# Two attention heads scored inside the value product, and relative biases asked for one head at a time

## The chip, the cores and the metric

The program runs on one core of a Trainium2 chip. Its time is the device time of one execution in microseconds (us). The kernel before took 2087.86 us, the median of three executions (2085.55, 2087.86 and 2088.91 us).

## The reference, cut to what matters

The model is two blocks one after the other, in f32, on 512 tokens of width 1024. The second block, which is the part that the change touches, has two layers. Each layer is attention, then a gated feed-forward network:

```python
for i in range(2):
    h = rmsnorm(x, norm_mix[i])
    # layer 0: 12 query heads, 4 key and value heads, a window of 128 tokens on either side,
    #          ALiBi slopes as biases and a sink logit per head
    # layer 1: 12 heads of query, key and value, a 16-column window on an 8 x 64 grid,
    #          relative biases rpb from a table
    s = einsum(q, k) * 64 ** -0.5 + bias        # masked outside the window
    y_tok = softmax(s) @ v
    y_mem = softmax(q_mem @ mk) @ mv            # 4 more heads on 256 memory tokens
    x = x + concat(y_tok, y_mem) @ w_out[i]
    h = rmsnorm(x, norm_ffn[i])
    x = x + (silu(h @ w_gate) * (h @ w_up)) @ w_down[i]
```

## The kernel before, in words

**Engines and queues.** Every engine has its own program, and they meet at semaphores. SyncE (SP) starts all DMAs. The weights come as a stream of numbered units, two buffers `raw[0]` and `raw[1]`. ScalarE (ACT) rounds a unit to `w_hi` (`split_hi`, L727), VectorE (DVE) makes the rest `w_lo` (`split_lo`, L1212), and TensorE (PE) multiplies three times for each tile: `w_hi` by `z_hi`, `w_hi` by `z_lo`, `w_lo` by `z_hi` (L1924 to L1936). SP may load unit N when `w_lo` of unit N-2 is done, and ACT may round unit N when PE is through with unit N-2. A unit of `qk` has 24 matmuls of 512 columns.

**Layer of the second block.** The stage `qk` makes queries and keys (10 units in layer 0, 14 in layer 1). ACT copies each unit's result from PSUM (L1143 to L1149), DVE multiplies it by the token's scale (L1776), ACT and DVE split it (L1126, L1788). The stage `v` makes the values: in layer 0 two units, in layer 1 two halves of four units each. Its product (L2405 to L2416) takes 12 matmuls for each of eight k tiles, of 256 columns in layer 0 and 384 in layer 1. At the end of a half ACT and DVE copy two blocks each of the result to `v_tok` (L1161, L1809) and report it on the semaphores `va` and `vd`.

**Attention as a pipeline over heads.** All engines go through `head_steps` (L437), from head 0 to head 18. In step h, PE makes the scores of head h in four blocks (`scores`, L2426, two matmuls a block), turns the exponentials of head h-2 (`turn`, L2440), and multiplies them by the values (`values`, L2451; block 3 of a head falls into the next step). DVE adds the bias, takes the row maximum (`biased`, L1823, a custom instruction and a read of its accumulator), and negates the maxima (`neg_max`, L1896 and L1899). ACT takes the exponentials (L1170) and copies turned blocks to `pts` (L1178). Three PSUM banks go round between the score blocks, so that scores of one block wait until the block three before has been read.

**Where the scores lie.** `ls` (three slots) and two of the three bias slots overlie `z_hi` and `z_lo` (L193 to L195), the operands of the value product. So nothing of the attention but the bias of head 0 can be made before that product is over: GpSimd (POOL) waits for it at L714, and PE's own order puts the first `scores` behind it (L2418 to L2488).

**The biases.** POOL makes one per head, from the slopes in layer 0 (L695) and from the table in layer 1 (L705). For layer 1 SP asks for each head's part of the table with eight DMAs (`bias_load`, L557). The first three heads are asked for in one go, between the second and the third weight unit of `qk1`:

```python
load(n, 0, cols(w, 0))
load(n + 1, 1, cols(w, P))
if l == 1:
    sp.wait_ge(used, n + 2)
    for r in range(3):
        bias_load(r, r)
with sp.Fori(0, qkw // (2 * P) - 1) as i:
    load(n + 2 * i + 2, 0, cols(w, i * (2 * P) + 2 * P))
```

At the start of `qk1` the norm is finished beside the first two units: PE sums squares after the first unit (L2036) and spreads the scale inside the second (L2046), and ACT copies the scale (L788) before it may copy the first results.

Of the kernel before, what the change touches and what calls it, by code (L numbers as in the profile page):

```python
# [12 lines left out]
P = 128  # L13
# [59 lines left out]
def build(nc, t):  # L73
# [3 lines left out]
    with ctx:  # L77
# [21 lines left out]
        minus = sb(fixed, "minus", [P, 4])  # L99
        raw = [sb(fixed, f"raw{i}", [P, SLOT]) for i in range(2)]  # L100
# [64 lines left out]
        at = [scratch + 5 * 4 * T1]  # L165
        mk = sb(at, "mk", [P, 2 * MH, NMEM])
# [23 lines left out]
        bias = [sb([scratch], "bias0", [P, GRID_R * (48 + 32 + 32)])]  # L190
# [3 lines left out]
        ls = [sb(at, f"ls{i}", [P, 4, 3 * P]) for i in range(3)]  # L194
        bias += [sb(at, f"bias{i}", [P, GRID_R * (48 + 32 + 32)]) for i in range(1, 3)]  # L195
# [199 lines left out]

        def y_slot(head):

            return chunked(y_heads[:, head // 2 * 2, :], 4)[:, :, head % 2 * HD:(head % 2 + 1) * HD]
# [38 lines left out]
        def head_steps(eng, step):  # L437


            for h in range(AH + 3):  # L440
                step(h, h % 3, h, h // 3)
# [47 lines left out]
        def _(sp):  # L489
# [114 lines left out]
        def _(pool):  # L604
# [77 lines left out]
            for l in range(2):  # L682
# [8 lines left out]
                def biases(h, g, r):  # L691
                    if l == 0:
                        if h >= 2:
                            pool.wait_ge(*s.at("ls", 4 * h - 8))
                        pool.tensor_tensor(bias[r][:, 0:3 * P], att_con[:, 0:3 * P],  # L695
                                           con[:, bass.ds(cc["slopes"] + h, 1)].to_broadcast([P, 3 * P]),
                                           ALU.mult).then_inc(s["bias"], 1)
                    else:
# [3 lines left out]
                        for v, (first, n) in enumerate(((1, 2), (0, 3), (0, 2))):  # L702
                            x0 = first * BC
                            mask = att_con[:, 3 * P + 48 * v + x0:3 * P + 48 * v + x0 + n * BC]
                            x = pool.tensor_tensor(  # L705
                                bias[r][:, at_:at_ + n * P].rearrange("p (n r c) -> p n r c", n=n, r=GRID_R),
                                rpb_raw[r][:, :, x0:x0 + n * BC].rearrange("p r (n c) -> p n r c", n=n),
                                mask.rearrange("p (n o c) -> p n o c", n=n, o=1)
                                    .to_broadcast([P, n, GRID_R, BC]), ALU.add)
# [16 lines left out]
        def _(act):  # L726
# [386 lines left out]
            def layer(l):  # L1113
# [40 lines left out]
                for half in range((1, 2)[l]):  # L1154
                    count, width = ((2, KVA * HD), (4, 384))[l]
                    for i in range(count - 1):
                        m = count * half + i
                        split_hi(n + m + 2, i % 2, WIDTHS[n + m + 2])
# [5 lines left out]
                    m = count * (half + 1) - 1  # L1164
                    split_hi(n + m + 2, 1, WIDTHS[n + m + 2])

                def exps(h, r, memory, blocks):
                    for b in blocks:
                        lo, width = span(memory, b)
                        act.activation(ls[r][:, b, lo:lo + width], ls[r][:, b, lo:lo + width], ACT.Exp,  # L1170
# [25 lines left out]
                head_steps(act, step)  # L1196
# [14 lines left out]
        def _(dve):  # L1211
# [546 lines left out]
            def layer(l):  # L1758
# [43 lines left out]
                for half in range((1, 2)[l]):  # L1802
                    count, width = ((2, KVA * HD), (4, 384))[l]
                    for i in range(count - 1):
                        m = count * half + i
                        split_lo(n + m + 2, i % 2, WIDTHS[n + m + 2])
# [6 lines left out]
                    m = count * (half + 1) - 1  # L1813
                    split_lo(n + m + 2, 1, WIDTHS[n + m + 2])
# [8 lines left out]
                def biased(h, r, b):  # L1823
# [3 lines left out]
                    dve.tensor_tensor_reduce(ls[r][:, b, lo:lo + width], banks(r + b)[:, 0:width],  # L1827
                                             bias[r][:, at_:at_ + width], 1.0, 3 * NEG, ALU.add, ALU.max,
                                             row_max[r][:, b:b + 1]).then_inc(s["ls"], 1)

                def taken(h, r, b):

                    dve.wait_ge(*s.at("s", 4 * h + (b + 1)))
                    dve.tensor_copy(ls[r][:, b, 0:NMEM], banks(r + b)[:, 0:NMEM]).then_inc(s["ls"], 1)

                def largest(h, r, b):
                    dve.wait_ge(*s.at("ls", 4 * h + (b + 1)))
                    dve.tensor_reduce(row_max[r][:, b:b + 1], ls[r][:, b, 0:NMEM], AX.X, ALU.max)\
                       .then_inc(s["max"], 1)

                def copy(h, memory, b):
# [3 lines left out]
                    dve.tensor_copy(pts[1][:, 0:width], ps[3][:, 1, 0:width]).then_inc(s["pd"], 1)  # L1845

                def step(h, r, n_, g):
# [47 lines left out]
                    if banded and l == 0:  # L1895
                        dve.scalar_tensor_tensor(neg_max[r][:, :], row_max[r][:, :], vec("sink", h), minus[:, :],  # L1896
                                                 ALU.max, ALU.mult).then_inc(s["neg"], 1)
                    elif front:
                        dve.scalar_tensor_tensor(neg_max[r][:, :], row_max[r][:, :], -2.0, row_max[r][:, :],  # L1899
                                                 ALU.mult, ALU.add).then_inc(s["neg"], 1)  # L1900
                head_steps(dve, step)
# [14 lines left out]
        def _(pe):  # L1916
# [473 lines left out]
            def layer(l):  # L2390
# [8 lines left out]
                count, kt, width = ((2, 4, KVA * HD), (4, 2, 384))[l]  # L2399
                for half in range((1, 2)[l]):  # L2400
                    if l == 0 or half:
# [15 lines left out]

                pe.wait_ge(*s.at("scaled", (10, 14)[l]))  # L2418
                pe.wait_ge(*s.at("q_lo", (8, 12)[l]))
                pe.wait_ge(*s.at("zero", 1))  # L2420
                if l:

                    pe.wait_ge(*s.at("va", 1))
                    pe.wait_ge(*s.at("vd", 1))

                def scores(h, r, n_, b, kv):  # L2426
                    memory = n_ >= QH
                    _, width = span(memory, b)
                    bank = banks(r + b)[:, 0:width]
                    if memory:  # L2430
                        x = pe.matmul(bank, q_mem[:, n_ - QH, b * P:(b + 1) * P], mk[:, MH * l + n_ - QH, :],  # L2431
                                      start=True, stop=True)
                    else:
                        lo = key_block(False, b, 0) * P
                        for keys, first in ((k_hi, True), (k_lo, False)):
                            x = pe.matmul(bank, q_pair[:, n_, b * P:(b + 1) * P], keys[:, kv, lo:lo + width],  # L2436
                                          start=first, stop=not first)
                    x.then_inc(s["s"], 1)

                def turn(h, r, memory, b):  # L2440
# [5 lines left out]
                    for j in range(width // P):  # L2446
                        x = pe.transpose(ps[3][:, b % 2, j * P:(j + 1) * P],  # L2447
                                         ls[r][:, b, lo + j * P:lo + (j + 1) * P], ident)
# [39 lines left out]
                head_steps(pe, step)  # L2488
# [109 lines left out]
```

## Time and profile before

| | |
|---|---|
| median of three executions | 2087.86 us |
| the profiled execution | 2088.28 us |
| its span | 2086.5 us |
| PE busy | 2047.6 us, 98% |
| DVE busy | 1091.2 us, 52% |
| ACT busy | 868.2 us, 42% |
| POOL busy | 182.4 us, 9% |
| mean granted clock of TensorE | 0.995 |
| DMA | 28.5% of 16 engines |

The span runs from the first to the last instruction that the profile sees; 1.8 us of the profiled execution lie outside it. In the rows below, a timeline row is: start in us, length in us, engine, line, operation, output from inputs, shape, count, and in brackets the engine's idle time just before it and what ended it. PE is matmuls and PEld the loading of stationary operands. Matmul ends are modelled, so that the next one may start before the end shown.

### The profile page before, as it was taken

To read this page: it belongs to the slowest core of one execution; us is meant where nothing else is said; L and a number is where in the kernel's file an instruction comes from. 1 tells how busy PE (TensorE), PEld (TensorE's weight loads), DVE (VectorE), ACT (ScalarE), POOL (GpSimd) and SP (SyncE) were. 2 spreads that over 40 slices of the span, in tenths; PEclk is the share of its full clock that TensorE was granted. 3 is DMA by queue.
4 is the path that set the end of the run, shared out by engine and by line. 5 is a ranking of instruction groups with operands and counts; after the bars stand their busy time and mean duration, and the time that the engine had idled before them with its cause. 6 is when DMAs were issued, how large, how long until landed. Compare 5 with 4: busy or idle time off the path is not lost.

```text
span 2086.5 us, 32286 instructions
## 1 busy us (share of the span) xinstructions
PE 2047.6 (98%) x11899; PEld 1793.3 (86%) x11899; DVE 1091.2 (52%) x1809; ACT 868.2 (42%) x1350; POOL 182.4 (9%) x177
## 2 busy tenths in 40 slices
PE   8999999999999999999999999999999999999998
PEld 8999999999988988888988888888789888888887
DVE  4234777555662566556764433444555654433443
ACT  5534444543221544456743322234556643322233
POOL 0013000110010000001000100010004001100000
PEclk9999999999999999999999999999999999999999
DMA  4322111133333333332023332332322033333332
GB/s 134 104 81 81 41 42 41 55 88 91 93 103 111 90 90 94 104 106 61 1 71 100 91 111 81 92 104 78 100 83 60 24 91 97 102 93 91 90 102 80
DMA packets 321921, 174.99 MB, mean 84 GB/s; under 512 B 6561, under 2 KB 319137, under 8 KB 321841
## 3 DMA queue, kind: packets, MB, share of 16 engines
q1 hardware_dynamic: 321840, 173.92, 28.5%
q8 instruction: 50, 0.82, 0.2%
q14 instruction: 31, 0.25, 0.0%
HBM read 171.80 MB, written 2.10 MB: 83 GB/s over the span
## 4 chain that ended last, share of the span: by engine, by line
PE 66%; DVE 1%; ACT 1%; DMA 1%; issue 1%; SPq 0%; POOL 0%; POOLq 0%; DVEq 0%; ACTq 0%
PE ps L1928 38%; PE ps L1934 19%; PE ps L2462 3%; PE ps L2414 2%; PE ps L2447 2%; PE ps L2436 1%; PE ps L2431 1%; SPq L561 0%; ACT w_hi L731 0%; PE ps L2496 0%; DVE w_lo L1214 0%; DMA raw<-w_in_a 0%; DMA raw<-w_mem_kv 0%; DMA raw<-w_in_b 0%; PE ps L2297 0%
## 5 line engine op out<-in xcount | busy, mean ns | idle before, releaser
L1928 PE MATMUL ps<-z_hi,w_hi 128*128 128x512 f32 (+2 forms) x2128 | 645.2, 344 | 7.7 <-ACT scaled_heads L1143 5.1
L1928 PE MATMUL ps<-z_lo,w_hi 128*128 128x512 f32 (+2 forms) x2128 | 635.9, 339 | 0.0
L1214 DVE TENSOR_TENSOR w_lo<-raw,w_hi 128x1024 fp32r<-128x1024 f32 (+2 forms) x298 | 384.1, 1289 | 467.5 <-ACT w_hi L731 466.3
L731 ACT ACTIVATE w_hi<-raw 128x1024 fp32r<-128x1024 f32 (+2 forms) x298 | 328.2, 1102 | 428.4 <-PE ps L1934 374.4
L1934 PE MATMUL ps<-z_hi,w_lo 128*128 128x512 f32 (+2 forms) x2128 | 443.8, 339 | 0.0
L1928 PEld LDWEIGHTS ps<-z_hi,w_hi 128*128 128x128 f32 x2128 | 367.2, 189 | 60.4 <-issue 10.4
L1928 PEld LDWEIGHTS ps<-z_lo,w_hi 128*128 128x128 f32 x2128 | 366.0, 189 | 45.0
L1934 PEld LDWEIGHTS ps<-z_hi,w_lo 128*128 128x128 f32 x2128 | 344.2, 188 | 45.3
L1928 PE MATMUL ps<-g_hi,w_hi 128*128 128x512 f32 (+1 forms) x539 | 209.4, 390 | 0.5 <-POOL g_lo L662 0.5
L1928 PE MATMUL ps<-g_lo,w_hi 128*128 128x512 f32 (+1 forms) x539 | 208.8, 389 | 0.0
L662 POOL TENSOR_TENSOR g_lo<-gv,g_hi 128x512 f32 x66 | 85.6, 1297 | 1075.2 <-ACT g_hi L1068 1075.2
L1934 PE MATMUL ps<-g_hi,w_lo 128*128 128x512 f32 (+1 forms) x539 | 147.4, 388 | 0.0
L1559 DVE TENSOR_TENSOR H<-H,ps 128x512 f32<-128x512 f32 (+2 forms) x64 | 44.1, 689 | 178.4 <-PE ps L1934 178.4
L1928 PEld LDWEIGHTS ps<-g_hi,w_hi 128*128 128x128 f32 x539 | 101.1, 188 | 23.9 <-POOL g_lo L662 1.9
L1928 PEld LDWEIGHTS ps<-g_lo,w_hi 128*128 128x128 f32 x539 | 101.2, 188 | 22.1
L1934 PEld LDWEIGHTS ps<-g_hi,w_lo 128*128 128x128 f32 x539 | 99.7, 188 | 21.9
L1068 ACT ACTIVATE g_hi<-gv 128x512 f32 (+1 forms) x66 | 41.7, 632 | 181.2 <-DVE gv L1702 181.2
L1928 PE MATMUL ps<-mix_hi,w_hi 128*128 128x264 f32 (+1 forms) x256 | 76.5, 339 | 0.0
L1928 PE MATMUL ps<-mix_lo,w_hi 128*128 128x264 f32 (+1 forms) x256 | 76.3, 339 | 0.0
L1170 ACT ACTIVATE ls<-ls,neg_max 128x256 f32<-128x256 f32 (+1 forms) x128 | 68.7, 539 | 6.7 <-DVE neg_max L1899 6.7
L2462 PEld LDWEIGHTS ps<-v_tok,pts 128*128 128x128 f32 x480 | 64.8, 192 | 3.1 <-DVE pts L1845 1.2
L2462 PE MATMUL ps<-v_tok,pts 128*128 128x64 f32 x480 | 64.8, 266 | 0.5 <-ACT pts L1178 0.5
(317 smaller groups left out, 2387.8 us busy)
## 6 DMA issues: line engine op xcount, KB each, us to landing
raw<-w_gate_up SPq DMA_DIRECT2D x88, 512.0 KB, 3.7
raw<-w_down SPq DMA_DIRECT2D x48, 704.0 KB, 4.4
raw<-w_in SPq DMA_DIRECT2D x44, 512.0 KB, 3.7
raw<-w_up SPq DMA_DIRECT2D x44, 512.0 KB, 3.7
raw<-w_out SPq DMA_DIRECT2D x24, 512.0 KB, 3.6
raw<-w_in_b SPq DMA_DIRECT2D x14, 512.0 KB, 3.8
raw<-w_in_a SPq DMA_DIRECT2D x12, 512.0 KB, 3.6
raw<-w_branch SPq DMA_DIRECT2D x8, 512.0 KB, 3.6
```

Of the source, the lines that this page charges most:

```text
L662: pool.tensor_tensor(lo, src, hi.bitcast(F32), ALU.subtract).then_inc(done, 1)
L731: act.activation(w_hi[s][:, 0:width], raw[s][:, 0:width], ACT.Copy).then_inc(hi_done, 1)
L1068: act.activation(g_hi[:, j, 0:tokens], gv[:, 0:tokens], ACT.Copy).then_inc(s["hi"], 1)
L1170: act.activation(ls[r][:, b, lo:lo + width], ls[r][:, b, lo:lo + width], ACT.Exp, bias=neg_max[r][:, b:b + 1], accum_out=row_sum[r][:, b:b ...
L1214: dve.tensor_tensor(w_lo[s][:, 0:width], raw[s][:, 0:width], w_hi[s][:, 0:width].bitcast(F32), ALU.subtract).then_inc(lo_done, 1)
L1559: dve.tensor_tensor(tile, tile, more, ALU.add).then_inc(ps_free[s], 1)
L1928: pe.matmul(out, w_hi[s][:, w0 + k * P:w0 + (k + 1) * P], rhs[:, lo:lo + width], start=a, stop=False)
L1934: x = pe.matmul(out, w_lo[s][:, w0 + k * P:w0 + (k + 1) * P], rhs_hi[:, lo:lo + width], start=False, stop=last)
L2414: x = pe.matmul(v_bank(l, half, c)[:, 0:width], zz[:, k, c * P:(c + 1) * P], ww[i % 2][:, kk_ * width:(kk_ + 1) * width], start=a, stop=b)
L2431: x = pe.matmul(bank, q_mem[:, n_ - QH, b * P:(b + 1) * P], mk[:, MH * l + n_ - QH, :], start=True, stop=True)
L2447: x = pe.transpose(ps[3][:, b % 2, j * P:(j + 1) * P], ls[r][:, b, lo + j * P:lo + (j + 1) * P], ident)
L2462: x = pe.matmul(y_bank(r)[:, b * HD:(b + 1) * HD], pts[b % 2][:, j * P:(j + 1) * P], v, start=j == 0, stop=j == width // P - 1)
```

## The change

Scores, bias and maxima of heads 0 and 1 are made inside the value product: PE puts one score block behind each of the eight k tiles (in layer 1 of the second half only), DVE handles the blocks ahead of its weight splits, and ACT takes the exponentials of head 0 ahead of copying the values. The steps of `head_steps` then start with head 2. For that, `ls` slots 0 and 1 and bias slot 1 move to other places, POOL makes the bias of head 1 before the product's end, and in layer 1 PE waits for `va` and `vd` of the first half ahead of the second. In the `qk` stage of layer 1, `bias_load` of heads 0, 1 and 2 goes ahead of the units 4, 6 and 8, one head each. The moves of `ls[r]` to `ls(r, b)` and `bias[r]` to `bias[l][r]` elsewhere are left out here.

```diff
+        tails = [fixed[0] + 4 * SLOT * i + 4 * UNIT for i in (0, 1, 4, 5)]
...
+        first_bias = sb([scratch], "bias0", [P, GRID_R * (48 + 32 + 32)])
+        ls_first = sb([scratch + 2 * 4 * T1], "ls0", [P, 4, 3 * P])
+        ls_second = [sb([tails[b]], f"ls1_{b}", [P, 3 * P]) for b in range(4)]
...
-                load(n, 0, cols(w, 0))
-                load(n + 1, 1, cols(w, P))
-                if l == 1:
-
-                    sp.wait_ge(used, n + 2)
-                    for r in range(3):
-                        bias_load(r, r)
-                with sp.Fori(0, qkw // (2 * P) - 1) as i:
-                    load(n + 2 * i + 2, 0, cols(w, i * (2 * P) + 2 * P))
-                    load(n + 2 * i + 3, 1, cols(w, i * (2 * P) + 3 * P))
+                for i in range(qkw // (2 * P)):
+                    if l == 1 and 2 <= i < 5:
+                        sp.wait_ge(used, n + 2)
+                        bias_load(i - 2, i - 2)
+                    load(n + 2 * i, 0, cols(w, i * (2 * P)))
+                    load(n + 2 * i + 1, 1, cols(w, i * (2 * P) + P))
...
                 biases(0, 0, 0)
+                biases(1, 0, 1)
 
                 pool.wait_ge(used, UNITS[f"out{l}"] + 2)
-                for h in range(1, QH):
+                for h in range(2, QH):
                     biases(h, h // 3, h % 3)
...
+                for half in range((1, 2)[l]):
+                    count, width = ((2, KVA * HD), (4, 384))[l]
+                    final = half == (0, 1)[l]
+                    for i in range(count):
+                        m = count * half + i
+                        if i == count - 1:
+                            if final:
+                                step(1, 1, 1, 0)
+                            values_taken(half, count, width)
+                        split_hi(n + m + 2, i % 2, WIDTHS[n + m + 2])
+                head_steps(act, step, 2)
...
+                def front_blocks(h, blocks):
+
+                    dve.wait_ge(*s.at("bias", h + 1))
+                    dve.wait_ge(*s.at("scaled", 2 * pairs))
+                    for b in blocks:
+                        scored(h, b)
+                        biased(h, h, b)
+                    if 3 in blocks:
+                        dve.wait_ge(*s.at("ls", 4 * h + 4))
+                        negated(h, h)
...
+                for half in range((1, 2)[l]):
+                    count, width = ((2, KVA * HD), (4, 384))[l]
+                    final = half == (0, 1)[l]
+                    for i in range(count):
+                        m = count * half + i
+                        if final:
+                            first = 8 * i // count
+                            front_blocks(first // 4, range(first % 4, first % 4 + 8 // count))
+                        if i == count - 1:
+                            values_taken(half, count, width)
+                        split_lo(n + m + 2, i % 2, WIDTHS[n + m + 2])
+                head_steps(dve, step, 2)
...
                 for half in range((1, 2)[l]):
+                    final = half == (0, 1)[l]
+                    if l and half:
+                        pe.wait_ge(*s.at("va", 1))
+                        pe.wait_ge(*s.at("vd", 1))
...
+                            if final:
+                                h, block = divmod(kt * i + kk_, 4)
+                                if k == 0:
+                                    pe.wait_ge(*s.at("q_lo", (8, 12)[l]))
+                                pe.wait_ge(*s.at("ls", 4 * h + (block - 2)))
+                                scores(h, h, h, block, (0, h)[l])
                         x.then_inc(used, 1)
...
-                head_steps(pe, step)
+                pe.wait_ge(*s.at("scaled", (10, 14)[l]))
+                pe.wait_ge(*s.at("zero", 1))
+                head_steps(pe, step, 2)
```

## Rows read from the trace of the kernel before

**Rows 1.** The page: PE's busy time, and the qk weight loads of layer 1.

```profile
PE 2047.6 (98%) x11899; PEld 1793.3 (86%) x11899; DVE 1091.2 (52%) x1809; ACT 868.2 (42%) x1350; POOL 182.4 (9%) x177
...
raw<-w_in_b SPq DMA_DIRECT2D x14, 512.0 KB, 3.8
```

**Rows 2.** PE's waits, whole span: line, released by; us in total, times, longest.

```profile
PE ps L2436 <- DVE row_max L1827: 5.5, 2, 3.0
```

**Rows 3.** Timeline of the start of qk1, SP, DVE and PE.

```profile
1457.32 11.03 SPq L561 DMA_DIRECT2D rpb_raw<-rpb  x24
...
1460.94 1.23 DVE L1214 TENSOR_TENSOR w_lo<-raw,w_hi 128x1024 fp32r<-128x1024 f32 x1
...
1466.36 1.05 PE L2046 MATMUL ps<-con,stat 128*128 128x128 f32 x8
...
1475.26 0.79 PE L1928 MATMUL ps<-z_hi,w_hi 128*128 128x512 f32 x1 [5.06 <-ACT scaled_heads L1143]
```

**Rows 4.** The chain of waits: start us, us, what, matmuls in it.

```profile
953.94 11.38 PE ps L2414 x96
...
1472.50 1.06 ACT w_hi L731
...
1475.26 6.45 PE ps L1928 x16
...
1483.57 3.69 PE ps L1928 x16
...
1546.58 33.40 PE ps L2414 x189
```

**Rows 5.** Timeline from the end of layer 0's value product.

```profile
965.02 0.19 PEld L2436 LDWEIGHTS ps<-k_hi,q_pair 128*128 128x128 f32 x1
...
965.34 0.88 DVE L1809 TENSOR_SCALAR v_tok<-ps,stat 128x256 f32<-128x256 f32 x2 [3.31 <-PE ps L2414]
...
965.38 1.61 POOL L695 TENSOR_TENSOR bias<-att_con,con 128x384 f32<-128x384 f32 x2 [13.27 <-PE ps L2414]
...
966.06 1.05 ACT L731 ACTIVATE w_hi<-raw 128x1024 fp32r<-128x1024 f32 x1
...
968.77 0.58 PE L2436 MATMUL ps<-k_hi,q_pair 128*128 128x256 f32 x1 [2.54 <-DVE row_max L1827]
...
969.61 0.43 DVE L1827 CUSTOM_DVE_ANT_0 ls<-ps,bias 128x256 f32<-128x256 f32 x1
...
977.19 0.55 PE L2462 MATMUL ps<-v_tok,pts 128*128 128x64 f32 x4
...
981.51 0.55 PE L2462 MATMUL ps<-v_tok,pts 128*128 128x64 f32 x4
```

**Rows 6.** Timeline of layer 1's value product: between the halves, and from its end.

```profile
1562.97 0.88 PE L2414 MATMUL ps<-w_hi,z_hi 128*128 128x384 f32 x4
1563.17 1.14 DVE L1809 TENSOR_SCALAR v_tok<-ps,stat 128x384 f32<-128x384 f32 x2 [2.30 <-PE ps L2414]
...
1579.62 0.19 PEld L2436 LDWEIGHTS ps<-k_hi,q_pair 128*128 128x128 f32 x1
...
1583.90 0.58 PE L2436 MATMUL ps<-k_hi,q_pair 128*128 128x256 f32 x1 [2.98 <-DVE row_max L1827]
...
1592.66 0.55 PE L2462 MATMUL ps<-v_tok,pts 128*128 128x64 f32 x4
```

**Rows 7.** Instructions of L1896: duration ns min/median/max, first and last start.

```profile
L1896 DVE SCALAR_TENSOR_TENSOR neg_max<-row_max,par,minus x12: 223/887/891, 970.1 to 1016.0; 128x4 f32<-128x4 f32 x12
```

**Rows 8.** Table by stretch: us, busy us of each engine, then PEclk, DMA share, GB/s.

```profile
868.00:875.00 7.00, 4.85 (x42) 4.68 (x41) 3.59 (x5) 3.22 (x6) 0.00 (x0) 1.00 0.38 120
...
968.70:972.00 3.30, 3.23 (x10) 2.60 (x10) 3.26 (x16) 1.00 (x4) 0.83 (x1) 0.50 0.54 159
...
1583.90:1586.90 3.00, 3.00 (x11) 2.75 (x12) 2.96 (x14) 1.11 (x5) 3.00 (x5) 0.50 0.23 50
```

**Rows 9.** Timeline of PE in the memory stage.

```profile
870.71 0.36 PE L1928 MATMUL ps<-mz_hi,w_hi 128*128 128x256 f32 x1 [2.15 <-DVE w_lo L1214]
```

More of the change, by code:

```diff
@@ L165, in build @@
         at = [scratch + 5 * 4 * T1]
+        mk_at = at[0]
         mk = sb(at, "mk", [P, 2 * MH, NMEM])
@@ L193, in build @@
         at = [fixed[0] - 2 * 4 * KD * T1]
-        ls = [sb(at, f"ls{i}", [P, 4, 3 * P]) for i in range(3)]
-        bias += [sb(at, f"bias{i}", [P, GRID_R * (48 + 32 + 32)]) for i in range(1, 3)]
+        ls_third = sb(at, "ls2", [P, 4, 3 * P])
+        last_bias = sb(at, "bias2", [P, GRID_R * (48 + 32 + 32)])
+        k_lo_unused = region + 4 * SEQ * (AH + QH + KVA)
+        bias = [(first_bias, sb([(k_lo_unused, mk_at)[l]], f"bias1_{l}", [P, GRID_R * (48 + 32 + 32)]), last_bias)
+                for l in range(2)]
         pts = [sb(at, f"pts{i}", [P, 3 * P]) for i in range(2)]
@@ L435, in key_block, with head_steps @@
             return j if memory else max(b - 1, 0) + j
-        def head_steps(eng, step):
-            for h in range(AH + 3):
+        def head_steps(eng, step, first=0):
+            for h in range(first, AH + 3):
                 step(h, h % 3, h, h // 3)
@@ L692, in biases @@
                     if l == 0:
-                        if h >= 2:
+                        if h >= 3:
                             pool.wait_ge(*s.at("ls", 4 * h - 8))
-                        pool.tensor_tensor(bias[r][:, 0:3 * P], att_con[:, 0:3 * P],
+                        pool.tensor_tensor(bias[l][r][:, 0:3 * P], att_con[:, 0:3 * P],
                                            con[:, bass.ds(cc["slopes"] + h, 1)].to_broadcast([P, 3 * P]),
@@ L1153, in layer, with values_taken @@
                 n = UNITS[f"v{l}"]
[L1154 to L1158, printed above, removed]
+                def values_taken(half, count, width):
                     act.wait_ge(used, n + count * (half + 1) + 2)
@@ L1169, in exps @@
                         lo, width = span(memory, b)
-                        act.activation(ls[r][:, b, lo:lo + width], ls[r][:, b, lo:lo + width], ACT.Exp,
+                        act.activation(ls(r, b)[:, lo:lo + width], ls(r, b)[:, lo:lo + width], ACT.Exp,
                                        bias=neg_max[r][:, b:b + 1], accum_out=row_sum[r][:, b:b + 1])\
@@ L1801, in layer, with values_taken @@
                 n = UNITS[f"v{l}"]
[L1802 to L1806, printed above, removed]
+                def values_taken(half, count, width):
                     dve.wait_ge(used, n + count * (half + 1) + 2)
@@ L1826, in biased @@
                     at_ = (0, 2 * P, 2 * P, 5 * P)[b] if l else lo
-                    dve.tensor_tensor_reduce(ls[r][:, b, lo:lo + width], banks(r + b)[:, 0:width],
-                                             bias[r][:, at_:at_ + width], 1.0, 3 * NEG, ALU.add, ALU.max,
+                    dve.tensor_tensor_reduce(ls(r, b)[:, lo:lo + width], banks(r + b)[:, 0:width],
+                                             bias[l][r][:, at_:at_ + width], 1.0, 3 * NEG, ALU.add, ALU.max,
                                              row_max[r][:, b:b + 1]).then_inc(s["ls"], 1)
@@ L1894, in step @@
                         dve.wait_ge(*s.at("max", 4 * (n_ - QH) + 4))
[L1895 to L1901, printed above, removed]
+                    if front:
+                        if banded:
+                            negated(h, r)
+                        else:
+                            dve.scalar_tensor_tensor(neg_max[r][:, :], row_max[r][:, :], -2.0, row_max[r][:, :],
+                                                     ALU.mult, ALU.add).then_inc(s["neg"], 1)
+                for half in range((1, 2)[l]):
[10 more added lines that the diff above has]
+                head_steps(dve, step, 2)
                 for k in range(KD):
@@ L2399, in layer, with scores @@
                 count, kt, width = ((2, 4, KVA * HD), (4, 2, 384))[l]
+                def scores(h, r, n_, b, kv):
+                    memory = n_ >= QH
+                    _, width = span(memory, b)
+                    bank = banks(r + b)[:, 0:width]
+                    if memory:
+                        x = pe.matmul(bank, q_mem[:, n_ - QH, b * P:(b + 1) * P], mk[:, MH * l + n_ - QH, :],
+                                      start=True, stop=True)
+                    else:
+                        lo = key_block(False, b, 0) * P
+                        for keys, first in ((k_hi, True), (k_lo, False)):
+                            x = pe.matmul(bank, q_pair[:, n_, b * P:(b + 1) * P], keys[:, kv, lo:lo + width],
+                                          start=first, stop=not first)
+                    x.then_inc(s["s"], 1)
                 for half in range((1, 2)[l]):
+                    final = half == (0, 1)[l]
+                    if l and half:
+                        pe.wait_ge(*s.at("va", 1))
+                        pe.wait_ge(*s.at("vd", 1))
                     if l == 0 or half:
@@ L2415, in layer @@
                                                   ww[i % 2][:, kk_ * width:(kk_ + 1) * width], start=a, stop=b)
-                        x.then_inc(used, 1)
[L2418 to L2438, printed above, removed]
+                            if final:
[4 more added lines that the diff above has]
+                                scores(h, h, h, block, (0, h)[l])
+                        x.then_inc(used, 1)
                 def turn(h, r, memory, b):
```

24 lines of the change are left out of this document (14 added, 10 removed).

## The prediction

> **What bounds the kernel now.** I read the page first. PE is busy for 98% of the span and no other engine for more than 52% [rows 1], so only what gives PE its idle or slow time back can move the end. Next come PE's waits: the longest kind is the first scores of attention behind DVE's row maxima, 5.5 us in two places, one per layer [rows 2], then one wait of 5.06 us at the start of qk1 [rows 3]. The timelines around these three places say what stands in the way, and the chain of waits and the table by stretch say what the clock did there: after each of the three idle times PE runs for some microseconds at half of its full clock (granted 0.50, that is 1.2 instead of 2.4 GHz) [rows 4, 8].
>
> **Start of qk1.** SP spends 11.03 us on 24 asks for relative biases [rows 3], 3.7 us a head. They are queued ahead of the third weight unit, which lands when ACT starts rounding it, at 1472.50 [rows 4]. PE starts on it at 1475.26 after 5.06 us idle, and its first 16 matmuls take 6.45 us where the next unit's take 3.69 [rows 3, 4]. They end at 1481.71.
>
> In the new order the third and fourth unit are asked for first. The third is asked for before the stage begins, the fourth at 1462.2, when the second unit's w_lo is done [rows 3]; each lands 3.8 us later [rows 1], so the DMA is early. What is late next is ACT: it copies the scale after PE has spread it, which ends at 1467.41 [rows 3]. From 1472.50 to 1475.26 ACT rounds (1.06), copies the scale and copies two heads [rows 4, 3]: 2.76 us, of which 1.70 follow the rounding. The rounding now fits ahead of the spread, so PE's bank is free at 1467.41 + 1.70 = 1469.1. PE is through with the second unit at 1470.0 (its modelled end is 1475.26 - 5.06 = 1470.20, and its next matmul can start a little earlier). So PE doesn't stop, the clock stays up, and the 16 matmuls end at 1470.0 + 3.7 = 1473.7. Gain 1481.7 - 1473.7 = **8.0 us**.
>
> The 24 asks don't vanish. Each group of eight (3.7 us) now stands on SP between unit 3 and 4, 5 and 6, 7 and 8. Between two loads of the stream lie about 5.5 us (24 matmuls at 3.69/16 = 0.231 us), so 3.7 us fit in. Even if a load went out late by all of 3.7 us, it would land 7.5 us after its release, and PE needs it only two units (11.1 us) less a split of about 2.5 us after the unit two before is through. I cost this at nothing; without that cover it would be 3.7 us less slack for each load, up to a few microseconds. POOL needs the first bias only at the end of qk1, 80 us on. The unrolled loop on SP costs nothing that PE sees.
>
> **Ramp of attention, layer 0.** Now the value product ends at 965.02, PE makes three score blocks and then stands for 2.54 us until DVE has copied the values, split a unit and freed a bank [rows 5]. Then DVE and ACT have to go through head 0 and head 1 before values can be multiplied, at half clock on PE. The steady state is visible in block 3 of the values: 977.19 for head 0, 981.51 for head 1, so 4.32 us a head [rows 5].
>
> Afterwards eight score blocks (16 matmuls) lie inside the product. By width one matmul takes 11.38/96 = 0.119 us at 256 columns and 33.40/189 = 0.177 us at 384 [rows 4], so a head's scores take 1.18 us, both 2.36. This work is moved, not added. The product's last matmul is issued by 965.02 + 2.36 - 0.24 = 967.14 (the last score block, 0.24, comes behind it). Call this E. At E + 0.35 ACT, DVE and POOL are released, as at 965.34 to 965.38 now [rows 5]. ACT copies (till E + 1.2) and rounds (1.05, till E + 2.3). DVE must first do the last block of head 1 (starts at E + 0.45, 0.43 and a read), then its neg_max, then the value copies of 0.88. POOL starts two biases at E + 0.36, 0.8 us each [rows 5], and neg_max takes 0.22 us alone but 0.89 beside such a bias in nearly all of its instances [rows 7]. I let it end with POOL's first bias, at E + 1.25; the bounds are E + 1.1 and E + 2.0 (behind the second one). The values are then there at E + 2.2, and PE starts step 2 there; step 2 waits for them at its head. From there to block 3 of head 0's values PE has one period, less that block (0.4), plus turn and scores of the next step (0.47): 4.4 us, and I add 0.4 for ACT's first copies, which stand behind exponentials. That is E + 7.0 = 974.1 against 977.19: gain **3.1 us**. DVE is the next to be late: its weight split (1.23) now follows ACT's rounding at E + 2.3, and its first block of head 2 comes at about E + 4.2, but PE needs it only for block 3 of step 2, at about E + 5.
>
> The skill bears on that delay. The Trainium skill, GPSIMD Engine Reference, Key points, says that GpSimd shares its SBUF interfaces with VectorE and contends with instructions that have two SBUF inputs; neg_max has two, the value copies read PSUM. By that rule the copies themselves run undisturbed (they took 0.88 beside POOL, so the trace agrees), and only neg_max delays them. Without any such contention the sum would be 0.2 us better.
>
> **Ramp, layer 1.** The same, with one added wait: PE may not start the second half before the first half's values are copied. DVE's copies run from 1563.17 for 1.14 us, while PE starts its second half at 1562.97 [rows 6]: **1.4 us lost**. Behind this wait stand only PE's own second half and all that follows. E is 1579.62 + 1.4 + 2.1 = 1583.1, values are copied at E + 2.35 (copies of 1.14), block 3 of head 0's values comes at E + 7.15 = 1590.3 against 1592.66 [rows 6]. Gain **2.4 us**, the 1.4 already paid.
>
> Inside the product the new DVE work stands ahead of the weight splits. In layer 1 a unit takes 24 x 0.177 + 0.6 = 4.8 us. Two blocks (1.0), a neg_max (0.2) and a split (0.96) are under 2.5, and the last block is ready 0.3 us after the unit. So the splits keep up, and I cost them at nothing; without cover each of two splits in layer 1 could hold PE by 1 to 2 us. ACT's four exponentials of head 0 and its table load, some 4 us, lie beside PE's last units in both layers.
>
> **Sum.** 8.0 + 3.1 + 2.4 = 13.5 us. The profiled execution took 2088.28, which gives 2074.8; the median of the runs shown is 0.4 lower, so **2074.4 us**.
>
> **Rivals.**
> - *The clock falls again in the new ramps* (chance 0.22). PE stands at both ramps once more: from the end of its last score (E + 0.4) to E + 2.2 or E + 2.35, 1.8 to 1.95 us, and up to 2.7 if POOL's second bias goes first. The clock fell after 2.54 and 2.98 us [rows 5, 6, 8], and stayed at 1.00 after 2.15 [rows 9, 8]. If it falls, PE, which now has its full load behind the gap, runs 3 to 6 us at half speed and loses 1.5 to 3 us in each layer: 13.5 less 3 to 6, so 2077.5 to 2080.5, or half of it if one layer is hit. The Trainium skill, TensorE: Matmul & The Clock Gate, What's actually happening, says that the activity monitor runs free of the kernel, so that the same gap need not cost the same in each run; no row here shows that.
> - *The ramps give nothing* (0.08), because DVE falls behind and catches up only slowly (it has about 0.5 to 1 us of slack in a head), and layer 1 pays for its wait. Then 8.0 and less remain: 2080 to 2082. Against it: nothing that PE needs from DVE is late in step 2 by the working above.
> - *The asks for biases only move the stall* (0.06): a load behind eight asks comes late, PE stops again and the clock falls. 5.5 from the ramps and 0 to 4 from qk1: 2079 to 2082.5. For it speaks that each ask is many small pieces; against it, the slack above.
> - *Slower than before* (0.03): in layer 1's second half. If the wait at its start is over 2.5 us instead of 1.4, and DVE's splits, now queued behind score blocks, hold PE a little in every unit, then PE's clock doesn't come back: 17 us of value product and 2.4 us of scores at half speed cost 19 more, and the time is about 2092 to 2094. The product runs at a full clock now, and a wait of 2.15 us didn't bring it down [rows 9, 8].
> - The two aims can't fail to take effect at all: the order of the queues is written out.
>
> **How the numbers follow.** My forecast has 0.61. Its own bounds are neg_max behind POOL (0.8 a layer), the first copies of the step (0 to 0.8 a layer), qk1 by 7 to 8, and 1.5 us of spread of the runs: 2072.3 to 2076.8. With the clock rival the range is 2072.3 to 2080.5, which leaves out some 0.15. A measurement of this kernel can tell about 0.2%, 4 us, from no change. All cases but the last are over that or near it: faster by over 0.2% (below 2083.7) 0.95, within 0.02, slower 0.03.
>
> **What would show it.** qk1: no wait of PE on scaled_heads, its clock at 1.00 from 1457 on, first eight asks behind the fourth load. Value product: scores between its matmuls, a wait of 1.4 us once, in layer 1. At its end an idle time of about 2 us that the v_tok copies of DVE release, neg_max just ahead of them, clock 1.00 behind it, and block 3 of head 0's values about 7 us after the product's last matmul. The forecast is wrong if PE's clock reads 0.50 in a ramp, if PE waits for w_lo in the value product, or if qk1 has a stall left.

## The result and the profile after

The changed kernel took **2074.63 us** (median of four executions, 2073.57 to 2075.85) beside 2087.99 us before (2085.55 to 2088.91): a ratio of 0.9939, 95% interval 0.9924 to 0.9954. The forecast was 2074.4. The profiled execution took 2073.57 us with a span of 2071.8, so it stands 14.7 us below the profiled one of before, 1.3 more than the medians do.

The page of the changed kernel, busy times first, and then PE's waits, longest in total first (engine, line, released by; us, times, longest):

```profile
span 2071.8 us, 32220 instructions
PE 2039.3 (98%) x11899; PEld 1787.6 (86%) x11899; DVE 1092.4 (53%) x1805; ACT 868.1 (42%) x1350; POOL 185.1 (9%) x177
```

```profile
PE ps L2492 <- issue: 3.9, 2, 2.0
PE ps L1970 <- DVE w_lo L1229: 3.5, 2, 2.1
...
PE ps L1970 <- DVE mv L1739: 2.0, 2, 1.2
PE ps L2474 <- ACT q_mem L1158: 1.7, 1, 1.7
PE ps L2474 <- ACT v_tok L1168: 1.3, 1, 1.3
```

The waits of [rows 2], 5.5 us in two places, and the one of 5.06 us at the start of qk1 [rows 3] are gone. In their place stand 3.9 us in two places at the head of step 2 (L2492 is `turn`), and 1.3 us ahead of the second half of layer 1's value product. PE is busy for 8.3 us less with the same number of matmuls [rows 1]. Of that, 7.7 us lie in the three stretches in which it ran at half clock before (2.1 in layer 0's ramp, 2.8 in the `qk` stretch, 2.8 in layer 1's).

**Start of qk1**, timeline, the counterpart of [rows 3]:

```profile
1458.33 3.75 SPq L573 DMA_DIRECT2D rpb_raw<-rpb  x8
...
1459.63 1.04 ACT L740 ACTIVATE w_hi<-raw 128x1024 fp32r<-128x1024 f32 x1
...
1462.02 1.05 PE L2088 MATMUL ps<-con,stat 128*128 128x128 f32 x8
1462.12 8.00 SPq L511 DMA_DIRECT2D raw<-w_in_b  x2
...
1463.11 0.60 ACT L797 ACTIVATE sig<-ps 128x512 f32<-128x512 f32 x1 [2.43 <-PE ps L2088]
1463.60 1.19 ACT L1152 ACTIVATE scaled_heads<-ps 64x512 f32<-64x512 f32 x2
```

ACT rounds the third unit ahead of the spread, as forecast, and frees PE's bank at 1464.8, 0.9 us before PE needs it. Eight asks take 3.75 us and fit between two loads.

**End of layer 0's value product**, timeline, the counterpart of [rows 5]:

```profile
952.72 0.63 PE L2474 MATMUL ps<-w_hi,z_hi 128*128 128x256 f32 x4
...
966.23 0.28 PE L2452 MATMUL ps<-k_hi,q_pair 128*128 128x256 f32 x1
...
966.48 2.39 POOL L703 TENSOR_TENSOR bias<-att_con,con 128x384 f32<-128x384 f32 x3 [13.66 <-PE ps L2474]
966.66 0.42 DVE L1838 CUSTOM_DVE_ANT_0 ls<-ps,bias 128x256 f32<-128x256 f32 x1 [1.08 <-PE ps L2452]
...
967.13 0.22 DVE L1861 SCALAR_TENSOR_TENSOR neg_max<-row_max,par,minus 128x4 f32<-128x4 f32 x1
...
967.27 0.87 DVE L1822 TENSOR_SCALAR v_tok<-ps,stat 128x256 f32<-128x256 f32 x2
968.25 1.70 DVE L1229 TENSOR_TENSOR w_lo<-raw,w_hi 128x1024 fp32r<-128x1024 f32 x1
968.46 0.41 PE L2492 MATMUL ps<-con,ls 128*128 128x128 f32 x2 [1.83 <-issue]
...
972.85 0.55 PE L2507 MATMUL ps<-v_tok,pts 128*128 128x64 f32 x4
```

**Layer 1's value product**, timeline, the counterpart of [rows 6]:

```profile
1552.27 0.93 PE L2474 MATMUL ps<-w_hi,z_hi 128*128 128x384 f32 x4 [1.28 <-ACT v_tok L1168]
...
1571.17 0.29 PE L2452 MATMUL ps<-k_hi,q_pair 128*128 128x256 f32 x1
...
1573.62 0.41 PE L2492 MATMUL ps<-con,ls 128*128 128x128 f32 x2 [2.04 <-issue]
...
1578.01 0.55 PE L2507 MATMUL ps<-v_tok,pts 128*128 128x64 f32 x4
```

I read the gain off three stretches, rows two to four of the table, each between the same two pieces of work in both traces. E is here the issue of the first matmul behind the product's last one (the prediction counts its E from the weight load ahead of that matmul, 0.12 us earlier in layer 0 and 0.17 in layer 1); block 3 of head 0's values is where the steady state has set in.

| stretch | before | after | gain |
|---|---|---|---|
| span's start to layer 0's value product | 953.77 | 952.72 | 1.05 |
| from there to block 3 of head 0's values, layer 0 | 23.42 | 20.13 | 3.29 |
| from there to layer 1's value product | 567.01 | 559.18 | 7.83 |
| from there to block 3 of head 0's values, layer 1 | 48.46 | 45.98 | 2.48 |
| from there to the end | 493.84 | 493.79 | 0.05 |

The first row is no part of the change: in the memory stage PE waited 1.84 us for `mv` at 898.30 before and 0.78 at 897.25 after, and in a later profile of the very same changed kernel (e10) 1.95 us. Without it the sum is 13.65 us; forecast was 13.5.

### The profile page after: what moved, and what is told of

It reads as the page before. It is cut to its first block, busy times and chain, and to the rows that moved or that the text cites. A ratio compares the mean times of both kernels' runs of the same rounds, so it can differ in the third digit from the quotient of the medians.

```text
span 2071.8 us, 32220 instructions
## 1 busy us (share of the span) xinstructions
PE 2039.3 (98%) x11899; PEld 1787.6 (86%) x11899; DVE 1092.4 (53%) x1805; ACT 868.1 (42%) x1350; POOL 185.1 (9%) x177
## 4 chain that ended last, share of the span: by engine, by line
PE 68%; DVE 1%; issue 1%; ACT 0%; DMA 0%; POOL 0%; POOLq 0%; DVEq 0%; ACTq 0%
PE ps L1970 39%; PE ps L1976 19%; PE ps L2507 3%; PE ps L2474 2%; PE ps L2492 2%; PE ps L2452 1%; PE ps L2447 1%; PE ps L2543 0%; PE ps L2426 0%; DMA raw<-w_mem_kv 0%; DVE w_lo L1229 0%; PE ps L2088 0%; PE ps L2339 0%; ACT w_hi L740 0%; PE ps L2078 0%
```

## The experiments

"Block 3" below is block 3 of head 0's values, and "the ramp" is the time from E to it.

**e1, the asks alone.** The kernel before, with the new order of loads on SP and nothing else:

```diff
-                load(n, 0, cols(w, 0))
-                load(n + 1, 1, cols(w, P))
-                if l == 1:
-                    sp.wait_ge(used, n + 2)
-                    for r in range(3):
-                        bias_load(r, r)
...
+                for i in range(qkw // (2 * P)):
+                    if l == 1 and 2 <= i < 5:
+                        sp.wait_ge(used, n + 2)
+                        bias_load(i - 2, i - 2)
```

> The kernel before with only the order of the asks changed: bias_load of heads 0, 1 and 2 ahead of weight units 4, 6 and 8 of qk1. If the two parts of the change add up, this part gives back the wait of 5.06 us and the half clock behind it: 7.8 us faster than before, no wait of PE on scaled_heads, clock 1.00 through qk1, both attention ramps as before (waits of 2.5 and 3.0 us on the row maxima). The rival, that the asks only move the stall, gives 0 to 4 us and a wait of ACT on the weights at a later unit.

Measured: 2080.82 us beside 2088.68, 7.9 us less (ratio 0.9958, 0.9941 to 0.9974). The middle stretch took 559.23 us instead of 567.01. Table by stretch of e1 (us, busy us of PE, PEld, DVE, ACT, POOL, then PEclk, DMA share, GB/s): qk1 from its third unit on, and the start of layer 0's ramp.

```profile
1459.40:1476.00 16.60, 16.60 (x82) 13.80 (x81) 8.79 (x14) 10.13 (x14) 1.80 (x1) 1.00 0.31 84
...
970.10:973.40 3.30, 3.24 (x10) 2.61 (x11) 3.26 (x15) 1.02 (x4) 0.83 (x1) 0.50 0.56 159
```

PE has no gap in qk1 and its clock stays at 1.00; the old ramps, at 0.50, are as they were. Layer 0's took 12.85 us from E to block 3 instead of 12.05, behind the same gap of 2.5 us and the same order of work, because the clock came back later (granted 0.50 still from 973.5 to 976.5, where it read 1.00 before). So the 3.29 us of the table depend by 0.8 us on which execution of the old kernel was profiled. This part is settled at 7.8 us.

**e2, the ramps alone.** The changed kernel with the loads of qk1 back as they were (the diff above, reversed).

> The changed kernel with the asks for the first three heads back in one go between units 2 and 4. If the parts add up, it is 5.8 us faster than before (3.3 in layer 0, 2.5 in layer 1) and 7.8 us slower than the changed kernel, with the wait of 5 us and the clock at 0.50 behind it back at the start of qk1. If the gain of the ramps depends on the asks (biases there earlier), it would be less than 4 us.

Measured: 2083.93 us beside 2088.68, 4.8 us less and not 5.8 (ratio 0.9979, 0.9969 to 0.9989). The stall came back as expected (5.04 us, middle stretch 566.86). The missing part is in the ramps: 8.23 us in layer 0 and 8.46 in layer 1, against 6.62 and 6.84 in the changed kernel, though PE's gaps are the same 1.83 and 2.04 us. Table by stretch of e2, behind the two gaps:

```profile
968.30:971.80 3.50, 3.41 (x18) 3.44 (x19) 2.63 (x7) 2.16 (x8) 0.50 (x1) 0.60 0.13 35
...
1582.80:1586.30 3.50, 3.46 (x18) 3.49 (x19) 2.27 (x6) 2.07 (x7) 3.50 (x4) 0.59 0.18 35
```

and of the changed kernel, behind the same two gaps:

```profile
968.50:972.00 3.50, 3.50 (x31) 3.50 (x32) 3.02 (x11) 3.10 (x11) 0.37 (x1) 1.00 0.13 39
...
1573.50:1577.00 3.50, 3.38 (x30) 3.41 (x30) 2.83 (x9) 2.94 (x10) 3.50 (x4) 1.00 0.16 39
```

PE does 18 matmuls in a stretch where the changed kernel does 30 and 31. My clock rival had happened, in an execution of the same code in the ramps.

**e3, all 24 asks in one go, but later.**

```diff
-                    if l == 1 and 2 <= i < 5:
+                    if l == 1 and i == 2:
                         sp.wait_ge(used, n + 2)
-                        bias_load(i - 2, i - 2)
+                        for r in range(3):
+                            bias_load(r, r)
```

> The changed kernel, but all 24 asks in one go ahead of unit 4 (11 us), instead of 8 each ahead of units 4, 6 and 8. My theory is that only units 2 and 3 had to go first: unit 4 is then asked for at about 1469.5 instead of 1462, lands at 1473, and PE needs it at 1476.7, so the time is that of the changed kernel within 1 us and no wait appears. The rival, that one head at a time is what matters, gives a wait of ACT on the weights of unit 4 that reaches PE: 2 to 5 us slower than the changed kernel, with the clock at 0.50 behind it.

Measured: 2075.54 us (ratio 0.9934, 0.9918 to 0.9951), within 1 us of the changed kernel, and no gap of PE in qk1; only ACT waited, 1.56 us for the fifth unit. That the third and fourth unit go first is what counts; one head at a time isn't needed. Its ramps took 6.62 and 8.39 us, so its second gap of 2.04 us cost the clock and the first didn't.

**e4, the late wait.** PE's wait for the first half's values moves to the first scores of the second half:

```diff
-                    if l and half:
-                        pe.wait_ge(*s.at("va", 1))
-                        pe.wait_ge(*s.at("vd", 1))
...
                                 if k == 0:
                                     pe.wait_ge(*s.at("q_lo", (8, 12)[l]))
+                                    if l:
+                                        pe.wait_ge(*s.at("va", 1))
+                                        pe.wait_ge(*s.at("vd", 1))
```

> The changed kernel, with PE's wait for the first half's values in layer 1 moved from the head of the second half to the first score block in it. The first half's results and the second half's lie in different banks, and only the scores reuse the former. Theory: the wait of 1.28 us before the second half goes and nothing takes its place, since the first scores come 2.1 us into the half: 1.4 us faster than the changed kernel. The rival, that DVE or ACT is then late for the splits or at the end of the product, gives back part of it there as a longer idle time before step 2.

Measured: 2074.22 us (ratio 0.993, 0.9913 to 0.9946), where the changed kernel has 0.9939: 0.4 us less in the medians and some 1.9 us less by the ratios, which is no clear gain in time, nor does it show that there is none. The wait did go: from the start of layer 1's product to E it took 37.64 us instead of 39.14, 1.50 less. The profiled execution lost it 2 us later, to the clock: layer 1's ramp took 8.38 us instead of 6.84, behind a gap of 2.04 us as before. Table by stretch of e4:

```profile
1572.50:1576.00 3.50, 3.45 (x17) 3.48 (x18) 2.38 (x6) 1.95 (x6) 3.50 (x4) 0.52 0.16 35
```

**e5, a longer gap.**

```diff
+                        if final and i == count - 1:
+                            dead = con[:, cc["pair_ones"]:cc["eps"]]
+                            dve.tensor_tensor(dead, dead, dead, ALU.mult)
                         if i == count - 1:
                             values_taken(half, count, width)
```

> The changed kernel with one instruction more on DVE ahead of the values' copies at the end of each final value product (it squares 720 dead columns, about 0.8 us, or up to 1.3 beside POOL). PE's idle times there grow from 1.83 and 2.04 us to some 2.7 and 2.9. If the clock falls after such a gap, as it did in the kernel before after 2.54 and 2.98, PE runs its full load at half speed behind it: granted clock 0.50 for some 3 us in each layer, and 4 to 8 us slower than the changed kernel in all. If the clock stays, only the two added instructions show: 1.6 to 2.5 us slower.

Measured: 2080.62 us (ratio 0.9961, 0.9946 to 0.9977), 6 us above the changed kernel. The added instruction took 0.90 us in layer 0 and 1.71 in layer 1, where I had expected at most 1.3. The gaps grew to 2.65 and 3.67 us (0.82 and 1.63 more), the ramps to 8.85 and 11.21 (2.23 and 4.37 more). So the ramps grew by 1.4 and 2.7 us more than the gaps did, and that I put down to the clock, which reads 0.56 and 0.50 behind them. Timeline of e5, PE behind the gaps, and its table by stretch:

```profile
969.14 0.66 PE L2495 MATMUL ps<-con,ls 128*128 128x128 f32 x2 [2.65 <-issue]
...
1577.33 0.66 PE L2495 MATMUL ps<-con,ls 128*128 128x128 f32 x2 [3.67 <-issue]
```

```profile
969.10:972.60 3.50, 3.46 (x17) 3.49 (x18) 2.62 (x7) 2.14 (x7) 0.41 (x1) 0.56 0.15 42
...
1577.30:1580.80 3.50, 3.47 (x17) 3.50 (x17) 2.07 (x6) 1.96 (x6) 3.50 (x4) 0.50 0.23 49
```

**e6, the values first.** DVE copies the values ahead of head 1's last block, and PE scores two blocks of head 2 before it waits for them:

```diff
-                            front_blocks(first // 4, range(first % 4, first % 4 + 8 // count))
+                            last_one = i == count - 1
+                            front_blocks(first // 4, range(first % 4, first % 4 + 8 // count - last_one))
                         if i == count - 1:
                             values_taken(half, count, width)
+                            if final:
+                                front_blocks(1, (3,))
...
                     if n_ == 2:
-
+                        for b in range(2):
+                            pe.wait_ge(*s.at("ls", 4 * h + (b - 2)))
+                            scores(h, r, n_, b, kv)
...
-                        if front:
+                        if front and (n_ > 2 or b > 1):
                             scores(h, r, n_, b, kv)
```

> The changed kernel with another order at the end of the final value product: DVE copies the values before the last score block and neg_max of head 1, and PE makes the first two score blocks of head 2 before it waits for the values. If PE's idle time there is what DVE's last block and neg_max ahead of the copies make of it, it falls from 1.83 and 2.04 us to about 0.5, and the kernel gets 0.7 to 1.2 us faster in all, the rest being held up by ACT, which rounds a weight unit before its first pts copy. If neg_max and the last block are needed as early as they stand, the wait only moves behind step 2 and the time stays.

Measured: 2072.66 us (ratio 0.9924, 0.9908 to 0.9939), 2 us below the changed kernel, more than the 0.7 to 1.2 expected. The ramps took 5.96 and 5.92 us, 0.66 and 0.92 less than its best ones, and in both the clock stayed up. The two edits, DVE's order and PE's two early score blocks, were not run apart. What is late next is ACT, as expected. Timeline of e6, PE in layer 1's ramp:

```profile
1572.76 0.74 PE L2495 MATMUL ps<-con,ls 128*128 128x128 f32 x5 [0.44 <-ACT v_tok L1168]
...
1573.93 0.63 PE L2510 MATMUL ps<-v_tok,pts 128*128 128x64 f32 x4 [0.44 <-ACT pts L1183]
```

**e7, both, and the last split later.** e4 and e6 together, and on ACT and DVE the last weight split of the value stage moved behind step 3:

```diff
-                        split_lo(n + m + 2, i % 2, WIDTHS[n + m + 2])
-                head_steps(dve, step, 2)
+                        if not final or i < count - 1:
+                            split_lo(n + m + 2, i % 2, WIDTHS[n + m + 2])
+                for h in (2, 3):
+                    step(h, h % 3, h, h // 3)
+                split_lo(n + m + 2, i % 2, WIDTHS[n + m + 2])
+                head_steps(dve, step, 4)
```

> The late wait of layer 1 and the new order at the product's end together, and with them the last weight split of the value stage moved on ACT and DVE behind step 3 of the attention. If ACT's and DVE's work ahead of the first pts copy is what is late next, values of head 0 start some 1 us earlier in each layer: 3 to 4 us faster than the changed kernel (1.4 of it the late wait), near 2071 us. If DVE has no room for a split of 1.23 us inside the steady state, half a microsecond or more comes back at step 3 or 4, and 2 us faster are left.

Measured: 2071.14 us (ratio 0.9916, 0.9902 to 0.9929), 2069.93 to 2071.94. The ramps fell to 5.46 and 5.73 us. As block 3 comes in step 3, a stall that the moved split makes later isn't in these two numbers; e9 is what shows it.

**e9, both without the later split.** e4 and e6 together, run beside the unedited changed kernel (e8, below).

> The changed kernel with the late wait of e4 and the order of e6, and the weight splits where the changed kernel has them. By e6 the new order leaves no gap of over 0.5 us at the product's end, so the clock can't fall in any execution, and the whole 1.4 us of the late wait come through, which e4 lost to a clock that fell: 2071.2 us or so, 3 to 3.5 faster than the changed kernel beside it, and within 0.5 us of e7 or up to 1 us above it. If e4's wait gives nothing for another reason, it stays at e6's 2072.7.

Measured: 2070.93 us (2070.82 to 2071.60; ratio 0.9917, 0.9904 to 0.9931), beside 2075.75 of the changed kernel, 4.8 us less, and no execution of the one reaches into those of the other. Expected were 3 to 3.5; where the rest comes from is not shown. The ramps took 5.98 and 5.92 us. So the later split of e7 gains 0.5 and 0.2 us there and nothing that the time shows; the stretch behind layer 0's ramp is 0.2 us longer in e7 (559.49 us) than in e9 (559.29). This version is faster than both kernels.

**e8 and e10, the changed kernel again; e11, e4's kernel again.** No edits; the question is whether the same gap costs the same each time.

> The changed kernel once more, without an edit, for a second profile of the same gaps. In the profiles so far PE's gap of 1.83 us at the end of layer 0's product left the clock at 1.00 three times (changed kernel, e3, e4) and took it down once (e2), and the gap of 2.04 us in layer 1 left it up once and took it down three times (e2, e3, e4). If that is chance from one execution to the next, this kernel's runs spread over some 3 us (2072.5 to 2076.5) with mean clocks from 0.997 to 0.999, and its profile may show a ramp at half speed with 1.6 us lost that the first one did not. If it hangs on the code around it, the profile shows both ramps at 1.00 again and the gaps cost nothing.

> A third profile of the changed kernel, without an edit. If the clock behind the gaps of 1.83 and 2.04 us is a matter of the single execution, one of its two ramps may read below 1.00 this time (block 3 of head 0's values 8.2 to 8.5 us after the product's last matmul instead of 6.6 to 6.8); if it hangs on the code, both read 1.00 for the third time.

> A second profile of the kernel of e4, without a further edit. In e4 layer 1's ramp ran at half speed and took 8.4 us. If that is a matter of the single execution it may take 6.8 now, and the execution is then 1.6 us faster than e4's profiled one but for other differences; if it hangs on the code, it takes 8.4 again.

Measured: e8 2075.75 us (2074.35 to 2076.82; ratio 0.9938, 0.9925 to 0.9952), e10 2076.78 and e11 2073.58 us (one execution each). Ramps in us, gaps 1.83 and 2.04 us in all of them:

| profile | layer 0 | layer 1 |
|---|---|---|
| changed kernel | 6.62 | 6.84 |
| e8, the same | 6.62 | 6.84 |
| e10, the same | 6.61 | **8.43** |
| e4 | 6.62 | **8.38** |
| e11, the same as e4 | **8.22** | 6.84 |
| e3 | 6.62 | **8.39** |
| e2 | **8.23** | **8.46** |

Timeline of e10, PE behind the gap in layer 1, and its table by stretch there:

```profile
1575.27 0.41 PE L2492 MATMUL ps<-con,ls 128*128 128x128 f32 x2 [2.04 <-issue]
```

```profile
1575.00:1578.50 3.50, 3.23 (x18) 3.26 (x19) 2.36 (x6) 2.27 (x9) 3.50 (x4) 0.70 0.16 35
```

One kernel, one gap in layer 1, and the clock stayed up in two profiled executions and fell in the third; e4's kernel lost it in layer 1 in one execution and in layer 0 in the other. So it is a matter of the single execution. In 14 gaps of this length it fell 6 times (2 of 7 in layer 0, 4 of 7 in layer 1), at 1.6 us each.

The two ramps are not the only place. PE's gap of 2.15 us in the memory stage [rows 9] stands in every run, and the clock stayed at 1.00 behind it in ten of the thirteen profiles and fell in three (e3, e6, e8). Table by stretch of the changed kernel in its first profile and in e8, behind that gap:

```profile
871.50:875.00 3.50, 3.50 (x33) 3.50 (x31) 0.23 (x1) 0.00 (x0) 0.00 (x0) 1.00 0.71 208
```

```profile
871.50:875.00 3.50, 3.50 (x19) 3.50 (x19) 0.49 (x1) 0.04 (x1) 0.00 (x0) 0.52 0.71 220
```

Its price can't be read off here, since PE's later waits in that stage (0.4 to 1.5 us at 883, 0.8 to 2.1 at 898) change from run to run as well.

## Why the prediction was right

- **Start of qk1: 8.0 forecast, 7.83 measured.** Each step held: the rounding ahead of the spread, the bank free at the forecast distance (2.8 us after the spread began, here 1464.8), the clock at 1.00. e1 shows the part by itself, and e3 bears out that the moved asks cost nothing: even 11 us of them in one go, behind the fourth unit, left PE without a gap.
- **Ramp, layer 0: 3.1 forecast, 3.29 measured.** With the table's E, the forecast makes 13.5 us of the product with its scores and 6.9 of E to block 3; measured were 13.51 and 6.62.
- **Two terms inside it were off, against each other.** DVE's part came as forecast: neg_max ended at 967.36, 1.24 us after the prediction's E (1.25 forecast), and the values were copied at 968.14 (2.0 us after it, 2.2 forecast); in layer 1 it was 1.25, and 2.30 against 2.35. But PE started 0.32 us after the copies' end in both layers, which the working put at nothing. The profile calls that issue, and several waits stand there in a row; in e6, where PE makes two score blocks ahead of them, it was 0.09 and 0.10 us, and no run took the waits apart. Against that, the 0.4 us that I had added for ACT's first copies were not needed: from PE's start to block 3 it took 4.39 us in both layers, where one period alone makes 4.4.
- **neg_max beside POOL.** It took 0.22 us in layer 0 and 0.16 in layer 1, as without POOL (0.22 at 960.26), though POOL worked. In all 17 places of this trace where neg_max overlaps work of POOL, it ends 0.02 us after the first bias that it overlaps (0.89 us at 972.77, POOL from 972.81 for 0.83), or, where less is left of that bias than neg_max's own 0.16 or 0.22 us, 0.06 to 0.11 us after it. At 967.13 and at 1572.08 POOL's first bias was about to end, at 967.30 and 1572.14. In e6 it came 0.42 us after the start of the second bias and took 0.42 us, to that bias's end at 968.80. Timeline of e6:

```profile
967.19 2.40 POOL L703 TENSOR_TENSOR bias<-att_con,con 128x384 f32<-128x384 f32 x3 [13.65 <-PE ps L2477]
...
968.40 0.42 DVE L1861 SCALAR_TENSOR_TENSOR neg_max<-row_max,par,minus 128x4 f32<-128x4 f32 x1
```

- So "I let it end with POOL's first bias" held, and cost next to nothing. One overlap in e6, at 1581.48, was not held at all; why is open. The Trainium skill, GPSIMD Engine Reference, Key points, says that GpSimd contends with VectorE instructions that have two SBUF inputs: the trace agrees for neg_max in this way, and for the weight split behind (1.70 us here, 1.23 for other splits of this size).
- **Ramp, layer 1: 2.4 forecast, 2.48 measured,** with 1.47 paid ahead of the second half (12.17 us of lead at the product's start, 10.70 at its second half) against 1.4 forecast. e4 took that wait away and 1.50 us with it.
- **The splits inside the value product** never held PE: there is no wait on w_lo among its matmuls. The rival that ends slower than before needed that, and a wait of over 2.5 us ahead of the second half that takes the clock down; the wait was 1.28 us, and the clock read 1.00 behind it.
- **The clock rival had 0.22 and was mis-sized.** The gaps were as forecast (1.83 and 2.04, forecast 1.8 to 1.95), but I read the three gaps of the trace before as a limit between 2.15 and 2.54 us. There is none that sharp: gaps of 1.83 and 2.04 took the clock down in 6 of 14 cases, and the gap of 2.15 itself in 3 of 13. Of the seven profiled executions with both gaps, five had a fall in at least one ramp. The price, 1.5 to 3 us a layer, was 1.6. The prediction's own sign of being wrong, a clock at 0.50 in a ramp, is absent in two profiles of the changed kernel and there in the third (e10). The Trainium skill, TensorE: Matmul & The Clock Gate, What's actually happening, says that the activity monitor runs free of the kernel; the pairs e8 and e10, and e4 and e11, each one kernel with the same gaps and another outcome, agree with it, where the prediction had no row for it.
- **Luck in the number.** One fall costs 1.6 us and so stays inside the forecast's bounds. That the median came within 0.3 us of 2074.4 is partly chance: the same kernel's median was 2075.75 in e8, and its one execution in e10 took 2076.78.
- The two parts add up: 7.9 (e1) and 4.8 (e2) make 12.6 in medians, 13.4 together. The 0.8 us missing are less than the intervals of the two ratios leave open (some 3.4 us either way for e1, 2 for e2). e2's profiled execution lost the clock in both ramps, but one execution doesn't explain a median of ten.

## What to carry to other kernels

When a pipeline is filled beside a dense stage, what remains at the seam is one gap; look for what stands on each engine ahead of the work that ends it, and put the copy that the other side waits for first (e6, e9). A gap on PE of some 2 us can have a price beyond its length, and one that comes and goes between executions: a saving of 1.5 us (e4) is plain in the stretch where it is made and not in a median of four executions, so read such an edit off its own stretch, and in more than one profile. In a queue of DMAs, what counts is which transfers are due first, not how the others are cut up (e3).

## What the runs showed that I had not expected

The same gap of PE, 1.83 or 2.04 us, in the same kernel left the clock at full speed in one execution and brought it to half in another, 6 of 14 times; gaps of 0.5 us (e6, e7, e9, six ramps) never did, gaps of 2.65 and 3.67 us (e5) both did. Length isn't all: in the memory stage a gap of 2.15 us did in 3 of 13, and PE's wait for `mv` at 898, where it was 1.8 us or more (five profiles, up to 2.05), never did. What decides it in the single execution, no run shows. The spread of the times doesn't tell the two kinds apart: it is 2.5 us in e8 and 1.4 in e4, with both gaps in the ramps, and 0.8 in e9 and 2.0 in e7, without them.
